# T1 of the down stage added on VectorE, second partials added into DRAM, products interleaved, and plain transfers of the later passes begun by ScalarE's queue

## The reference

```
h2 = rmsnorm(x, ffn_pre_g)
up = causal_depthwise_conv(h2 @ w_up, conv_f_w, conv_f_b)     # 2 x 5632 columns, 3 taps
u_gate, u_val = jnp.split(up, 2, axis=-1)
f = (jax.nn.gelu(u_gate, approximate=True) * u_val) @ w_down   # (512 x 5632) @ (5632 x 2048)
x = x + rmsnorm(f, ffn_post_g)
e = (p[i] @ w_ple) * jax.nn.sigmoid(x @ w_ple_gate)
x = x + rmsnorm(e, ple_post_g)
```

## Time and profile before

| | |
|---|---|
| median of three runs | 2586.01 us (2580.02 to 2586.61) |
| the profiled execution | 2584.03 us, span 2582.2 us |
| granted TensorE clock, mean | 0.993 of full speed |
| busy | TensorE 98%, its weight load 86%, VectorE 70%, ScalarE 39%, GpSimd 8% |
| the down stage | from 1900.2 to 2355 us of the span |
| transfers | 432 MB, mean 167 GB/s; in the down stage 246 to 295 GB/s by pair |

### The profile page before, as it was taken

One profiled execution on the slowest core, in us unless ns is written; L12 is line 12 of the kernel. 1 busy time (PEld: TensorE's weight loads), 2 busy tenths in 40 slices (PEclk: granted clock), 3 DMA queues, 4 the chain that ended last, 5 costly groups with the idle time before them and its releaser, 6 DMA issues. The chain is left out here.

```text
span 2582.2 us, 36184 instructions
## 1 busy us (share of the span) xinstructions
PE 2523.4 (98%) x14322; PEld 2218.1 (86%) x14322; DVE 1805.8 (70%) x2194; ACT 1019.7 (39%) x1188; POOL 207.8 (8%) x291
## 2 busy tenths in 40 slices
PE   8999999999999999999999999999999999898998
PEld 7888888888888888799999999999987788676886
DVE  5888766653334236889989999899987776677534
ACT  5222322252223224444444444444454444445323
POOL 0000000000000000011110111111120111310000
PEclk9999999999999999999999999999999999999999
DMA  5333333333333323477777777777796988985221
GB/s 164 104 97 98 98 98 98 90 114 98 98 98 130 126 96 137 143 200 205 213 193 218 207 206 215 202 201 216 203 320 199 293 261 251 329 205 214 96 98 66
DMA packets 258798, 432.35 MB, mean 167 GB/s; under 512 B 13236, under 2 KB 162396, under 8 KB 257628
## 3 DMA queue, kind: packets, MB, share of 16 engines
q1 hardware_dynamic: 220480, 291.54, 33.9%
q0 software_dynamic: 35248, 134.23, 21.7%
q10 hardware_dynamic: 2924, 4.54, 0.5%
HBM read 393.30 MB, written 36.96 MB: 167 GB/s over the span
## 5 line engine op out<-in xcount | busy, mean ns | idle before, releaser
L1023 ACT ACTIVATE w_hi<-ring_raw 128x1024 fp32r<-128x1024 f32 x426 | 450.3, 1059 | 603.7 <-PE ps L926 387.5
L1429 DVE TENSOR_TENSOR ring_lo<-ring_raw,w_hi 128x1024 fp32r<-128x1024 f32 x426 | 518.9, 1221 | 221.8 <-ACT w_hi L1023 220.2
L1418 DVE TENSOR_TENSOR w_lo<-w_raw,w_hi 128x1024 fp32r<-128x1024 f32 x194 | 236.8, 1223 | 408.8 <-ACT w_hi L1013 408.5
L1013 ACT ACTIVATE w_hi<-w_raw 128x1024 fp32r<-128x1024 f32 x194 | 204.9, 1059 | 527.3 <-PE ps L717 387.1
L715 PE MATMUL ps<-xg_hi,w_hi 128*128 128x512 f32 x1024 | 400.7, 391 | 0.7 <-DVE w_lo L1418 0.6
L717 PE MATMUL ps<-xg_hi,w_lo 128*128 128x512 f32 x1024 | 399.2, 390 | 0.0
L716 PE MATMUL ps<-xg_lo,w_hi 128*128 128x512 f32 x1024 | 399.1, 390 | 0.0
L924 PE MATMUL ps<-s_hi,w_hi 128*128 128x256 f32 x1280 | 362.2, 283 | 3.2 <-issue 3.2
L926 PE MATMUL ps<-s_hi,ring_lo 128*128 128x256 f32 x1280 | 362.2, 283 | 0.0
L925 PE MATMUL ps<-s_lo,w_hi 128*128 128x256 f32 x1280 | 361.8, 283 | 0.0
L924 PE MATMUL ps<-xg_hi,w_hi 128*128 128x256 f32 x960 | 271.0, 282 | 0.4 <-DVE ring_lo L1429 0.4
(11 more groups left out here) (242 smaller groups left out, 4199.0 us busy)
## 6 DMA issues: line engine op xcount, KB each, us to landing
ring_raw<-in_w_up SPq DMA_DIRECT2D x200, 512.0 KB, 4.9
w_raw<-in_w_in SPq DMA_DIRECT2D x112, 512.0 KB, 3.8
ring_raw<-in_w_down SPq DMA_DIRECT2D x110, 512.0 KB, 7.2
ring_raw<-in_w_up POOLq DMA_DIRECT2D x80, 512.0 KB, 6.2
ring_raw<-in_w_down POOLq DMA_DIRECT2D x44, 512.0 KB, 8.7
w_raw<-in_w_o SPq DMA_DIRECT2D x32, 512.0 KB, 3.6
ring_raw<-in_w_ple_gate SPq DMA_DIRECT2D x32, 512.0 KB, 3.6
xd_raw<-gx_dram POOLq DMA_DIRECT2D x14, 1024.0 KB, 11.3
```

Source lines behind the costliest of these rows:

```text
L1023: f(w_hi[:, (U_S + n) % SLOTS], raw_of(n), ACT.Copy).then_inc(hi_ready, 1)
L1418: dve.tensor_tensor(w_lo[:, s], w_raw[:, u.slot(RAW)], as_f32(w_hi[:, s]), ALU.subtract).then_inc(lo_ready, 1)
L1429: dve.tensor_tensor(low_of_unit(n), raw_of(n), as_f32(w_hi[:, (U_S + n) % SLOTS]), ALU.subtract).then_inc(lo_ready, 1)
```

## The change

- **T1 on VectorE.** From pair 1 on, T1's second load is left out. VectorE adds W11's raw weight to T1's before W11's is split (`first_down`, 18 additions of 128x1024); the 4 of pair 0 stay with GpSimd.
- **Interleaved products.** From pair 1 on, W11 of a quad stands before W22, T1 and T2 of the same quad, not all W11 first. In pairs of 4 quads, pair 0 too, the last 12 units stand in the order T3 0, T3 1, W21 0, T4 0, T3 2, W21 3, T4 3, T3 3, W21 1, T4 1, W21 2, T4 2.
- **Partials.** Pass 0's four sums of a half are stored by ScalarE's queue; pass 1's are added into the same place in DRAM by GpSimd's queue; one plain load by ScalarE's queue brings both back. 16 stores, 8 loads and 8 adding loads become 8 stores, 8 adding stores and 8 loads.
- **Blocks of passes 1 and 2** are loaded by ScalarE's queue, W11, W22, T1 and T2 behind units 12 to 15 of the pair before (T1's and T2's pieces for the last pass behind its last T3 unit), T3, W21 and T4 behind units 1, 3 and 5 of the pass itself. `PREPARED` is set anew to suit.
- **Blocks of pass 0**: W21's and T4's loads go from unit 0 to units 8 and 10, T3's from 7 to 6.
- **End of the stage**: the reloads of `x2` are spread over four units, and `p_raw` comes before `gain_f`.

```
+def pair_units(p, h):
+    quads = PASSES[p]
+    if p + h == 0:
+        units = [(W11, q) for q in range(quads)]
+        units += [(mat, q) for q in range(quads) for mat in (W22, T1, T2)]
+    else:
+        units = [(mat, q) for q in range(quads) for mat in (W11, W22, T1, T2)]
+    if quads < 4:
+        return units + [(T3, q) for q in range(quads)] + [(mat, q) for q in range(quads) for mat in (W21, T4)]
+    return units + [(T3, 0), (T3, 1), (W21, 0), (T4, 0), (T3, 2), (W21, 3), (T4, 3), (T3, 3), (W21, 1), (T4, 1), (W21, 2), (T4, 2)]
...
 def adds(n):
-    return 1 if mat_of(n) in (T1, T3) else 0
+    return 1 if mat_of(n) == T3 or mat_of(n) == T1 and n < N_DOWN + START(0, 1) else 0
...
-            PREPARED.update({at + 10: (p + 1, W11), at + 19: (p + 1, W22)})
...
+            PREPARED.update({at + 18: (p + 1, W11), at + 20: (p + 1, W22)})
+            PREPARED.update({at + 22: (1, T1), at + 24: (1, T2), at + 37: (1, T3)} if p == 0 else
+                            {at + 25: (2, T1), at + 26: (2, T2), at + 35: (2, T3)})
+            PREPARED.update({at + 39: (p + 1, W21), at + 41: (p + 1, T4)} if p == 0 else {at + 37: (2, W21), at + 39: (2, T4)})
...
 # GpSimd
+                pool.wait_ge(c_out[buffer], 16 * (h + 1))
+                to = part_dram[h, k].rearrange("p (a f) -> p a f", a=2)
+                pool.dma_start(to, cb[buffer][:], accum_op=ALU.add).then_inc(c_added[buffer], 16)
...
-                if i == 0:
-                    load_blocks(0, W21)
-                    load_blocks(0, T4)
...
-                if i == 7:
+                if i == 6:
                     pool.wait_ge(gx_out[0], g_stored(QUADS - 1))
                     load_blocks(0, T3)
...
+                if i == 8:
+                    load_blocks(0, W21)
+                if i == 10:
+                    load_blocks(0, T4)
...
 # ScalarE
+                if h == 1 and nxt < len(PASSES):
+                    if at == bounds(p, h, W11)[1]:
+                        load_blocks(nxt, W11)
...
+                    if at == bounds(p, h, T3)[1] and spread_pieces(nxt, T1):
+                        load_blocks(nxt, T1)
+                        load_blocks(nxt, T2)
...
+                for k in range(4):
+                    if i == START(1, 1) + 17 + 3 * k:
+                        part_in(0, k)
+                    if i == START(2) + 6 + 3 * k:
+                        part_in(1, k)
...
 # VectorE
+            def first_down(n):
+                dve.wait_ge(ring_in[SLOT[n]], landed(n))
+                dve.wait_ge(ring_in[SLOT[n + 2]], landed(n + 2))
+                dve.wait_ge(units_done, U_S + PREVIOUS[n + 2] + 1)
+                dve.tensor_tensor(raw_of(n + 2), raw_of(n + 2), raw_of(n), ALU.add).then_inc(sum_ready, 1)
```

157 lines of the change are left out of this document (84 added, 73 removed).

## The result

| | before | changed |
|---|---|---|
| median, 12 runs each | 2584.27 us (2580.02 to 2586.75) | 2592.28 us (2589.27 to 2597.05) |
| the profiled execution, its span | 2584.03, 2582.2 | 2595.45, 2593.7 |

The ratio is 1.0029, with a 95% interval from 1.0021 to 1.0037: the change makes the kernel 8 us slower. The forecast was 2582, its range ended at 2592.

What follows compares the result with a forecast made beforehand. It took TensorE's 31.5 us of down-stage losses, mainly waits for weight splits and PSUM copies, as all that could be won. 2584.0 - 16.9 + 2.2 - 2.4 + 7.0 + 2.0 + 6.1 = 2582.0 us, range 2572 to 2592.

Steps and rivals of the forecast that it cites:

- the upper case: Pair 0: W21's block goes ahead in GpSimd's queue, the T3 addition lands at 1949, idle 13.5 us; lower bound 8.4.
- the clock's 2.0: Pairs 1 to 3: their three idles bring none to three drops to TensorE's lower clock at 1.6 us; +2.0 taken.
- -16.9 + 2.2: Pair 4: 13.66 us of waits and two clock drops go, -16.9; lateness of new things adds +2.2.
- What is late next there: Pair 4 after its waits go: 0.2 us before W21, as in undisturbed pair 5, and two new things.
- the 2.2 us for two new things: Pair 4: late T1 and T2 pieces and three T3 additions in a row, 1 us for either; +2.2 in the sum.
- Three T3 additions in a row: Pair 4: lateness from three successive T3 additions, taken as 1 us.
- Rival three: Pair 4: transfers stay the bound, over a third of the 16.9 stays, 6.5 us; 2588.5 us, chance 0.13.
- issues 34 transfers at some 0.3 to 0.5 us each: ScalarE: issuing its transfers fits in its idle time of 29 to 41 us busy per pair; priced at nothing.
- Rival two: Last units of pair 3: ScalarE waits for its own transfers, TensorE stands 12 us; 2596 us, chance 0.12.
- The chain in front of W21: Pairs 1 to 3: split and PSUM copies, 4.95 us, with one unit over them; idle 2.2, 2.6, 2.2, sum +7.0.
- The 20.5 us of VectorE's additions: Pairs 1 to 5: 18 T1 additions at about 1.14 us, covered by VectorE's slack, at nothing.
- Pair 1's 2.4 us: Pair 1: small waits go because T3 additions and W21 splits are now spread; -2.4.

Runs made afterwards that it cites:

- e10: e9 with the last pass's three 768 KB blocks issued at unit 24 of pair 3 and units 0 and 1 of pair 4: 2567.64 us, ratio 0.9940.
- e12: e10 with pair 4's three copies out of PSUM put in front of VectorE's split of the third T3 unit: 2566.21 us, ratio 0.9925.
- e9: Changed kernel with e3's copies, pair 0's block loads back where they were and the old order of the last 12 units in pair 0: 2569.43 us.
- e5: e3 with the second half's four partial loads at units 18, 20, 22, 24 from pair 4's start, not 6, 9, 12, 15: 2577.74 us.
- e4: Changed kernel with ScalarE's four block loads in pairs 1 and 3 behind units 12, 14, 16, 18, not 12 to 15: 2589.98 us.
- e1: Changed kernel with the old order of the last 12 units in pairs 0 to 2: 2588.31 us, ratio 1.0017.
- e3: Changed kernel with the three copies out of PSUM directly behind unit 15 in pairs of 4 quads: 2577.17 us, ratio 0.9973.
- e7: e3 with the 18 T1 additions of pairs 1 to 5 back on GpSimd's queue: 2580.66 us, ratio 0.9985.
- e11: Kernel before with second partials added in DRAM and the sum loaded once, later in pair 4, all on GpSimd's queue: 2574.96 us, ratio 0.9969.
- e13: e11 and e8 in one, on the kernel before: 2565.68 us, ratio 0.9920.
- e8: Kernel before with only the three copies of pairs of 28 units put directly behind unit 15: 2577.70 us, ratio 0.9972.

## Why the prediction was wrong

**The steps against the measurement**, by pairs, in us:

| pair | forecast | measured | what differed |
|---|---|---|---|
| 0 | +6.1 | +8.2 | the upper case; within its bounds of 8.4 and 13.5 for the idle (1.62 + 10.97) |
| 1 | -2.4 + 2.2, and a third of the clock's 2.0 | +4.5 | ScalarE's hold-up, 4.73 instead of 2.02 idle, and the lower clock behind it |
| 2 | +2.6, a third of 2.0 | +2.9 | nothing |
| 3 | +2.2, a third of 2.0 | +4.0 | 2.09 idle and a drop of the clock behind it |
| 4 | -16.9 + 2.2 | -7.2 | 0.98 + 6.81 idle and a drop of the clock |
| 5 | 0 | 0 | nothing |

**The step that failed is pair 4**: "What is late next there is what pair 5 shows in an undisturbed state, 0.2 us before W21", and the 2.2 us for two new things. -14.7 was forecast, -7.2 measured: 7.5 of the 13.4 us by which the profiled execution came out above the forecast. That the three waits of 13.7 us go was right. But 7.8 us of idle came in their place, with a unit of 5.0 instead of 2.75 us. Two things made them.

The larger is the lateness of the T3 additions. "Three T3 additions in a row" was priced at 1 us. They land 4.9 and 4.5 us apart, the third at 2278.1, and its split on VectorE has the chain of 9.5 us behind it even with no block in it. Pair 5 hides that chain, for its additions land in time. In pair 4 it doesn't fit: 2279.3 + 9.5 is 5 us behind the time at which W21 could have started, 2283.7 (2290.46 - 6.81). The smaller is the place of VectorE's work. I compared pair 4 with pair 5 and wrote that "in pairs 4 and 5 the order is as before". The last nine units are (the first twelve are interleaved); VectorE's work between them isn't. `PREPARED` puts the splits of the last pass's W21 and T4 blocks at units 9 and 11 of pair 4 (at + 37 and + 39), where they were at units 6 and 8. T4's now stands in the row without a gap, right in front of the copies, the same mistake of place that I did see for pair 0. By the two chains, 11.15 against 9.47 us, it costs 1.7 of the 6.8 us. No run moved it alone.

Earlier blocks cured the wait of the T3 unit, not that of W21 (e10); earlier copies cured W21's and left a shorter one at T3 (e12). The two took pair 4 from 67.6 (e9) to 64.7, where an undisturbed one would take 59. Why the additions land so far apart in pair 4 stays open: neither the partials' loads (e5) nor the blocks (e10) were it alone.

Rival three had the outcome for pair 4 (over a third of the 16.9 stays), and its time of 2588.5 was nearer than the forecast's; its mechanism, three queues on the same engines, is borne out in part only: T3's additions did stay late, but e5 took one queue's four loads away and nothing moved, and e10, with three blocks earlier, won 0.6 us in the pair.

**The second step that failed is that ScalarE "issues 34 transfers at some 0.3 to 0.5 us each", priced at nothing.** One of them took 5.38 us. Rival two looked for ScalarE's waits at the end of pair 3, where the six pieces in fact landed in 2.7 to 5.6 us, and not at the place where it issues four loads of 1 MB in four units. e4, with the four loads apart, has no such start, and pair 1 is 3.9 us shorter. So the hold-up was 2.7 us of idle and a longer stretch at the lower clock.

**What was right.** The chain in front of W21: 2.2 to 2.6 us forecast for pairs 1 to 3, and 2.02 (in e4), 2.58 and 2.09 measured; e1 and e3 take it away from either end. Pair 0's bounds; the queue's part came at its upper case, and the middle that went into the sum was 1.6 us of idle too low. The 20.5 us of VectorE's additions beside other work: e7, without them, is no faster in any pair. Pair 1's 2.4 us went as well, but not for the reason given, that the T3 additions and W21 splits are spread: e1 has the old order there and 76.7 us. The clock was undersized: 2.0 over three pairs; the units behind the idles of pairs 1 and 3 took 5.28 and 4.21 us, 2.5 and 1.5 too many, and after pair 2's longer idle there was no drop.

**The reading of the earlier trace rows was half right.** GpSimd's queue was backed up, but I put the cure to T1's additions and to moving transfers off the queue. e7 has T1's additions back and no T1 wait, and e11 leaves all on one queue and has only 3.5 us of it: taking loads of partials out of the front of pair 4 was enough. The additions land in 12.8 us in e11, and in 9.4 in e7, with three queues. The Trainium skill, "DMA: Bandwidth & Descriptors", section "Issuing engines are not separate DMA queues", says that issuing on several engines saves only issue time. By the time of the kernel it was nearer to the truth here than I made it: e13, all on one queue, is as fast as e12 with three. But the two differ in more than that (pair 4 is 1.8 us shorter in e12, pair 2 is 2.6 longer), so what the split is worth by itself wasn't measured. The earlier trace rows still stand against its letter: 23.2 us on one engine beside 8.2 on another.

**Open.** Pair 2 is 78 to 81 us in every kernel that stands on the changed one, and 76.9 in before, e8, e11 and e13. Where the copies are early, a part of it is a wait of 0.6 to 1.8 us for the split of the pair's second unit. e7 has 0.8 of it, so T1's additions on VectorE aren't needed for it; it also has 2.3 us in front of W21. Whether it is the interleaved order or the new places of the block splits was not tried. Nor was it tried how the hold-up of ScalarE depends on the bytes that are under way.

## What to carry to other kernels

When a unit is moved forward, move what frees its operands with it: the new order cost 2 to 5 us of idle in each of pairs 1 to 3 until the copies out of PSUM were moved too, and then nothing in pairs 1 and 3. When a place is called undisturbed, check that what arrives there arrives in time: pair 5 hid a chain of 9.5 us that pair 4, with late additions, did not. Test the parts of a bundled change alone and in pairs; here one part carried the gain, and a pair with two causes side by side didn't move until both were gone. When a queue is backed up, first see which transfers could be dropped or issued later, before moving some to another engine.
